# Two cross attentions by heads, an interleaved feature layout, and x's features ahead of the context's

## The chip, the cores and the metric

One core of a Trainium2 chip runs the whole program in one launch. The metric is the device time of that launch in microseconds (us). The kernel is written by hand for each engine: TensorE (PE in the profile, its weight loads PEld), VectorE (DVE), ScalarE (ACT), GpSimd (POOL, which issues the irregular transfers) and SyncE (SP, which issues the weight transfers). Engines meet at semaphores only, and each engine executes its own list of instructions in order.

## The reference, cut to what matters

256 tokens of width 2048 pass through two blocks. The first block has two layers; each projects x and a context, runs a gated attention beside a gated unit, and ends in an output product (`w_out`). In its first layer both x (2 tiles of 128 tokens) and the context (2 tiles) go through the output product; its second layer starts from the normed x:

```python
h = rms_norm(x, norm_w[layer]) * (1.0 + scale) + shift
proj = h @ w_in[layer]
...
x = x + gate * y
```

The second block has two layers, each a mixer, a cross attention to a memory of 256 tokens, and a feed-forward product with squared ReLU. The cross attention has 4 heads of width 128 (queries 2048 -> 512, outputs 512 -> 2048):

```python
x = x + memory_cross_attention(rms_norm_2(x, norm_xattn[layer]), rms_norm_2(mem, norm_mem[layer]),
                               xattn_wq[layer], xattn_wkv[layer], xattn_wo[layer])
x = x + squared_relu_mlp(rms_norm_2(x, norm_ffn[layer]), ffn_up[layer], ffn_down[layer])
```

Keys and values of the memory are computed earlier and lie ready in a DRAM buffer. Everything is float32. The large products are done with split operands: an operand is written as a rounded part (hi, of type fp32r) and the rest (lo), and a product is hi*hi + hi*lo + lo*hi, three matmuls.

## The kernel before, in words

**Weights.** All weights stream through `ring`, 8 slots of 2 x 128 rows x 512 columns (512 KB). SP loads slot u as soon as use u - 8 has been read by PE (`ring_free` for all but a product's last slot of a chunk, `gemm_full` for that one). ACT rounds a landed slot (`round_hi`, L1698), DVE subtracts (`take_lo`, L2542) and counts `w_lo`; PE waits for that count. In their instruction lists ACT and DVE do this one ring (8 uses) ahead of the use at which they stand.

**Products.** `gemm` (L917) goes chunk by chunk (512 columns of output) and, in a chunk, slot by slot; in a slot it takes every tile of 128 tokens, with the features as the stationary operand and 512 weight columns as the moving one, three matmuls for each of 2 rows of blocks. Output banks are the four `acc` banks; transposes and small products use the four `tp` banks in turn. `parts=True` makes every second slot of the first chunk wait for `feat_part`, the count of feature groups (4 of 16 blocks of 128 channels each) that are ready.

**Cross attention (`xat`, L1459, L2288, L3621).** The query product is one chunk of 8 slots for 2 tiles. After its 4th slot PE turns the last quarter of x (`turn_x`), after its 6th the keys (`turn_k`). ACT scales the two result banks by the tokens' norms into `xa_q` (L2296) and copies the turned keys. PE transposes the queries (L1476), DVE copies them to `xa_qt` (L3628). Then `attend` runs 8 units (2 token tiles x 4 heads): scores (L1048), row maximum on DVE (L2691), exponential on ACT (L1845), transposes of the probabilities (L1010), a copy on ACT (L1858), the product with the values (L1063), a scaling by the reciprocal sum on DVE. The outputs are transposed again, split by ACT (L1769) and DVE (L2616), and feed the output product `g_o`: 4 chunks of 2 slots, 2 tiles. DVE adds each chunk to x and takes the turned x of the chunk before into `feat`, the features of the feed-forward product.

**Feed-forward, upward product (`up_chunk`, L1484).** Here the weights are stationary and the features move: for each block of 128 weight columns a bank holds hi and lo of the result side by side. One matmul has 512 columns (w_hi against hi and lo of the features), one has 256 (w_lo against hi). hi and lo of `feat` are two arrays of 4096 columns each, so that the 512 columns are two runs of 256.

**From layer one to layer two of the first block.** The output product of layer one (4 tiles, 4 chunks of 8 slots) carries riders: each slot of the chunks 1 to 3 brings one more slot, of `w_mod`, which DVE sums up (L2526). In the last chunk PE turns three quarters of the new x as it stands before the norm (`turn_raw`, after the slots 2, 4 and 6); after the last slot it reduces the rider's sum (L1084), turns the last quarter and, once DVE has the diagonal of norms, spreads the norms over a bank (L1274). DVE's `x_features` (L2951) then multiplies the turned x by them (L2957), adds the shift (L2959), ACT rounds (L2063), DVE subtracts (L2591), in groups of 2, 2, 4, 4 and 4 blocks. Layer two's first product starts when the first two groups are done. ACT's list has the squares of all four tiles, then the root, before that (`sum_parts`).

Of the kernel before, what the change touches and what calls it, by code (L numbers as in the profile page):

```python
# [30 lines left out]
ACT = mybir.ActivationFunctionType  # L31
# [5 lines left out]
P = 128  # L37
# [6 lines left out]
KS = 2  # L44
# [151 lines left out]
def two_blocks(nc, I, out):  # L196
    ctx = ExitStack()
    with ctx:
# [28 lines left out]
        pairs[4096, KT * SEQ] = [feat_pair[:, j * KT * SEQ:(j + 1) * KT * SEQ] for j in range(2)]  # L227
        feat_both = feat_pair[:, :].rearrange("p (a k t) -> p a k t", a=2, t=SEQ)
# [92 lines left out]
        feat = pair(4096, KT, SEQ)  # L321
        hid_t = pair(12288, FFN // 2 // P, SEQ)
        HID = [v[:, :, :].rearrange("p b (j t) -> p b j t", t=SEQ) for v in (stage, prob)]
        rstd2 = att_s[:, 12:12 + TT]
        xn2 = view(16384, TT, D)
# [149 lines left out]
        xa_q = view(12288, TT, 512)  # L475
# [3 lines left out]
        xa_o = view(26624, TT, 512)  # L479
        xa_ot = pair(27648, 4, SEQ)  # L480

        def xat_units():
            return [dict(q=xa_qt[:, h, t * P:(t + 1) * P], k=xa_kt[:, h, :],
                         v=[xa_kv[:, j, 512 + h * HD:512 + (h + 1) * HD] for j in range(TT)],
                         out=xa_o[:, t, h * HD:(h + 1) * HD], gated=False, bias=None)
                    for t in range(TT) for h in range(4)]

# [115 lines left out]
        up_turns = []  # L603
        UP_BLOCKS = CH // P
# [277 lines left out]
        def _(pe):  # L882
# [34 lines left out]
            def gemm(g, lhs, hook=None, parts=False, late=None, between=None, each=None):  # L917
# [8 lines left out]
                def chunk(c, i, j0, s0, slots=range(g.slots)):  # L926

                    width = g.cols[c][1]
                    for s in slots:
# [9 lines left out]
                        for t in range(g.tiles):  # L939
# [266 lines left out]
            def block1(l):  # L1206
# [55 lines left out]
                def beside_out(c, s):  # L1262
                    if c == 3 and s in (2, 4, 6):
                        turn_raw(s // 2 - 1)
                    if c and s == g_out.slots - 1:
                        reduce_sum(summing[1, c])

                if l == 0:
                    gemm(g_out, feat_lhs(feat4), parts=True, each=beside_out)
                    turn_raw(3)  # L1270
# [5 lines left out]
                    tp_given["raw_ready"] += len(X_GROUPS)  # L1276
                else:
# [180 lines left out]

            def xat(l):  # L1459
                g_q, g_o = gemms[f"xat{l}"]  # L1460
                g_prev = gemms["odd" if l else "even"][-1]

                def turn_k(c, s):
                    if s != 5:
                        return
                    pe.wait_ge(sem("mem_in"), 16 * (5 + l))
                    for t in range(TT):
                        n, bank = tp_bank("act_tp")
                        for j in range(4):
# [3 lines left out]
                gemm(g_q, feat_lhs(feat), parts=True, between=(3, lambda: turn_x(g_prev, x4, 3)), each=turn_k)  # L1473
                pe.wait_ge(sem("xqk_ready"), E.due("xqk_ready"))
                for t in range(TT):
                    turn([xa_q[:, t, j * P:(j + 1) * P] for j in range(4)])  # L1476
                pe.wait_ge(sem("qkt_ready"), E.due("qkt_ready"))
                attend(xat_units())
                for t in range(TT):
                    pe.wait_ge(sem("src_ready"), E.due("src_ready"))  # L1480
                    turn_direct([xa_o[:, t, j * P:(j + 1) * P] for j in range(4)])
                gemm_to_x(g_o, feat_lhs(xa_ot), x4, parts=True)

            def up_chunk(g, c, parts, beside):  # L1484

                nonlocal q
                even = c % 2 == 0
                banks = []
                for s in range(g.slots):
                    slot = g.group(c, s)[0] % RING  # L1490
                    pe.wait_ge(sem("w_lo"), g.w0 + g.seq.index((c, s)) + 1)
                    if parts and KS * s % 4 == 0:
                        pe.wait_ge(sem("feat_part"), E.due("feat_part"))
                    for n in range(UP_BLOCKS):
                        if s == 0:
                            banks.append((None, begin("dve_free")) if even else tp_bank("tp_free"))
                        both = banks[n][1][:, :].rearrange("p (a t) -> p a t", a=2)
                        for k in range(KS):
                            kk = KS * s + k
                            w_hi, w_lo = (ring_r[:, slot, j, k, n * P:(n + 1) * P] for j in range(2))  # L1500
                            if kk == 0:
                                pe.matmul(both, w_hi, feat_both[:, :, kk, :], start=True, stop=False)  # L1502
                            mm = pe.matmul(both[:, 0], w_lo, feat_both[:, 0, kk, :], start=False, stop=False)  # L1503
                            if kk:
                                mm = pe.matmul(both, w_hi, feat_both[:, :, kk, :], start=False, stop=kk == g.kt - 1)  # L1505
                        if s == g.slots - 1:
# [2393 lines left out]
```

## Time and profile before

| | us |
|---|---|
| median of 3 runs (lowest to highest) | 3926.79 (3918.25 to 3931.02) |
| the profiled execution | 3919.9 |
| its span in the profile | 3917.9 |
| PE busy | 3774.4 (96%) |
| DVE busy | 2513.1 (64%) |
| ACT busy | 1610.7 (41%) |

The profile records one execution. Busy time of PE counts overlapping matmuls to their modelled ends, so the distance from one start to the next tells the pace, not the length of one. A timeline row is: start, length, engine, line, operation, out<-in, shape, count of merged instructions, and in brackets the idle time before it and what ended that.

### The profile page before, as it was taken

The page shows a single profiled execution, that of the slowest core. Times are in us where ns is not written, and L with a number is a line of the kernel's source. Part 1 is how long each engine was busy: PE and PEld are TensorE (multiplying, and loading weights), DVE is VectorE, ACT ScalarE, POOL GpSimd, SP SyncE. Part 2 cuts the span into 40 slices and gives each one's busy share as a digit, 9 for nine tenths or more (in the row PEclk, how much of TensorE's full clock was granted, in tenths as well). Part 3 has the DMA queues.
Part 4 walks back from the last instruction along what each step waited for, and adds up shares of the span by engine and source line. Part 5 has one row for each costly group of instructions (what it writes and reads, how often), then busy time and mean ns, then how long its engine had stood idle before and what let it go on. Part 6 is the DMA issues. An engine that isn't in the chain of part 4 may idle for free. (4 is left out here: it accounts for less than half of the span.)

```text
span 3917.9 us, 50221 instructions
## 1 busy us (share of the span) xinstructions
PE 3774.4 (96%) x20593; PEld 3052.9 (78%) x20593; DVE 2513.1 (64%) x3680; ACT 1610.7 (41%) x2274; POOL 151.8 (4%) x244
## 2 busy tenths in 40 slices
PE   7999999999999999989999999999989999999998
PEld 3688887787887887546878888888878878888887
DVE  7877786577776565766756644655496656545654
ACT  3322233324434443523445434444444554434443
POOL 2000000000000011022100000000000000000000
PEclk9999999999999999999999999999989999999999
DMA  9666564255762577244546656655645646556664
GB/s 377 231 207 202 185 196 161 81 178 155 264 204 98 190 242 222 67 152 136 179 129 183 189 193 193 190 192 189 223 143 162 218 129 190 190 193 191 189 204 156
DMA packets 352581, 722.44 MB, mean 184 GB/s; under 512 B 24064, under 2 KB 26436, under 8 KB 347488
## 3 DMA queue, kind: packets, MB, share of 16 engines
q1 hardware_dynamic: 331872, 637.74, 50.5%
q0 software_dynamic: 18784, 79.22, 5.9%
q8 instruction: 163, 2.67, 0.3%
q10 hardware_dynamic: 1696, 2.26, 0.2%
q14 instruction: 66, 0.54, 0.0%
HBM read 689.34 MB, written 26.37 MB: 183 GB/s over the span
## 5 line engine op out<-in xcount | busy, mean ns | idle before, releaser
L2542 DVE TENSOR_TENSOR ring_r<-ring,ring_r 128x1024 fp32r<-128x1024 f32 (+1 forms) x984 | 1189.0, 1217 | 1011.6 <-ACT ring_r L1698 1001.5
L1698 ACT ACTIVATE ring_r<-ring 128x1024 fp32r<-128x1024 f32 (+1 forms) x984 | 1030.9, 1054 | 1611.0 <-DMA ring<-in_w_in 412.0
L962 PE MATMUL acc<-ring_r,feat_hi 128*128 128x512 f32 x2688 | 834.9, 392 | 5.6 <-DVE feat_lo L2591 5.3
L962 PE MATMUL acc<-ring_r,hid_t_hi 128*128 128x512 f32 x2048 | 630.8, 389 | 0.0
L962 PEld LDWEIGHTS acc<-ring_r,feat_hi 128*128 128x128 f32 x2688 | 505.4, 189 | 116.2 <-issue 11.5
L962 PE MATMUL acc<-ring_r,feat_lo 128*128 128x512 f32 x1344 | 525.0, 391 | 0.0
L962 PEld LDWEIGHTS acc<-ring_r,hid_t_hi 128*128 128x128 f32 x2048 | 384.3, 188 | 79.4
L962 PE MATMUL acc<-ring_r,hid_t_lo 128*128 128x512 f32 x1024 | 398.5, 389 | 0.0
L1505 PE MATMUL tp<-feat_pair,ring_r 128*128 128x512 f32 x960 | 336.7, 394 | 0.0
L1505 PE MATMUL acc<-feat_pair,ring_r 128*128 128x512 f32 x960 | 336.4, 394 | 0.0
L962 PEld LDWEIGHTS acc<-ring_r,feat_lo 128*128 128x128 f32 x1344 | 253.7, 189 | 53.5
L1503 PE MATMUL acc<-feat_pair,ring_r 128*128 128x256 f32 x1024 | 274.0, 278 | 0.0
L1503 PE MATMUL tp<-feat_pair,ring_r 128*128 128x256 f32 x1024 | 273.9, 278 | 0.0
L962 PE MATMUL acc<-ring_r,feat_e_hi 128*128 128x512 f32 (+1 forms) x832 | 249.0, 382 | 1.1 <-DVEq L2618 1.1
L962 PEld LDWEIGHTS acc<-ring_r,hid_t_lo 128*128 128x128 f32 x1024 | 192.2, 188 | 40.0
L1505 PEld LDWEIGHTS tp<-feat_pair,ring_r 128*128 128x128 f32 x960 | 180.1, 188 | 39.3
L1505 PEld LDWEIGHTS acc<-feat_pair,ring_r 128*128 128x128 f32 x960 | 180.1, 188 | 39.0
L1503 PEld LDWEIGHTS tp<-feat_pair,ring_r 128*128 128x128 f32 x1024 | 192.4, 188 | 5.7
L1503 PEld LDWEIGHTS acc<-feat_pair,ring_r 128*128 128x128 f32 x1024 | 192.3, 188 | 5.4
L2526 DVE SCALAR_TENSOR_TENSOR big<-ring,silu_c,big 128x512 f32<-128x512 f32 x255 | 177.4, 746 | 29.0 <-DMA ring<-in_w_mod 27.9
L962 PEld LDWEIGHTS acc<-ring_r,feat_e_hi 128*128 128x128 f32 x832 | 154.1, 189 | 31.0 <-issue 1.3
L962 PE MATMUL acc<-ring_r,feat_e_lo 128*128 128x512 f32 (+1 forms) x416 | 158.8, 382 | 0.0
(520 smaller groups left out, 4395.6 us busy)
## 6 DMA issues: line engine op xcount, KB each, us to landing
ring<-in_ffn_up SPq DMA_DIRECT2D x256, 512.0 KB, 3.6
ring<-in_ffn_down SPq DMA_DIRECT2D x256, 512.0 KB, 3.6
ring<-in_w_mod SPq DMA_DIRECT2D x192, 512.0 KB, 4.8
ring<-in_w_in SPq DMA_DIRECT2D x176, 512.0 KB, 3.9
ring<-in_w_out SPq DMA_DIRECT2D x64, 512.0 KB, 3.8
ring<-in_even_w_in SPq DMA_DIRECT2D x64, 512.0 KB, 4.4
ring<-in_xattn_wkv SPq DMA_DIRECT2D x32, 512.0 KB, 4.4
ring<-in_even_w_out SPq DMA_DIRECT2D x32, 512.0 KB, 4.6
```

The source lines that it names most:

```text
L962: mm = pe.matmul(bank[0:l.shape[-1], 0:width], l, r, start=(kk == 0 and j == 0), stop=(kk == g.kt - 1 and j == len(terms) - 1))
L1503: mm = pe.matmul(both[:, 0], w_lo, feat_both[:, 0, kk, :], start=False, stop=False)
L1505: mm = pe.matmul(both, w_hi, feat_both[:, :, kk, :], start=False, stop=kk == g.kt - 1)
L1698: f(ring_r[:, slot, 0, 0:kt, 0:width], ring[:, slot, 1, 0:kt, 0:width], ACT.Copy) \
L2526: op = stt(v, w, by, v, ALU.mult, ALU.add)
L2542: tt(lo, raw, hi, ALU.subtract).then_inc(sem("w_lo"), E.up("w_lo"))
```

## The change

Three edits.

1. **Layout.** `feat` now holds hi and lo of a block of channels side by side: 16 blocks of (hi 256, lo 256). The 512 moving columns of the upward product are one run.
2. **Cross attention by heads.** The query product has the weights stationary, as the upward product has (`turned_block`): four banks, one for each head, come out as head x tokens, hi beside lo. The first four slots are done for all heads; from then on head by head (slots 4 to 7 of head 0, then 1, 2, 3), with the scores of heads 0 and 1, the transposes of head 0's probabilities and so on placed between. Query copies and transposes go away; the norms of the tokens enter as the exponential's scale. Scores of a head lie for both tiles in one `tp` bank; maximum, reciprocal and scaling are done for both tiles, the scaling on the probabilities. The product with the values has the values stationary, so that its output is already turned. The output product starts with slot 0 of its chunks 0 and 1, which need heads 0 and 1 only.
3. **x ahead of the context.** In the last chunk of layer one's output product, slots 4 to 7 are done for x's tiles first, and then for the context's. The remaining turns of x, the rider's sum, the norms and `x_features` are placed between the context's slots on PE, and between the weights' groups on ACT and DVE; the shift goes into ACT's rounding (as its bias) and into DVE's subtraction, one block of 256 columns at a time. The context's norm diagonal moves to the start of layer two.

```diff
-        feat_both = feat_pair[:, :].rearrange("p (a k t) -> p a k t", a=2, t=SEQ)
+        feat_both = feat_pair[:, :].rearrange("p (k a t) -> p k a t", a=2, t=SEQ)
...
+        feat = Pair(feat_both[:, :, 0], feat_both[:, :, 1], view(4096, KT, 2, SEQ)[:, :, 1])
+        feat_hl = feat_pair[:, :].rearrange("p (k n) -> p k n", n=2 * SEQ)
...
-            g.append(Gemm(f"xq{l}", W("xattn_wq_2", l), D, chunks(0, 512), 2, "act_free"))
+            g.append(Gemm(f"xq{l}", W("xattn_wq_2", l), D, chunks(0, 512), 4, "dve_free"))
```

PE, the product used by the queries and by the upward product:

```diff
+            def turned_block(g, bank, c, s, n, parts=False):
...
+                for k in range(KS):
+                    kk = KS * s + k
+                    w_hi, w_lo = (ring_r[:, slot, j, k, n * P:(n + 1) * P] for j in range(2))
+                    if kk == 0:
+                        pe.matmul(bank[:, :], w_hi, feat_hl[:, kk, :], start=True, stop=False)
+                    mm = pe.matmul(bank[:, 0:SEQ], w_lo, feat.hi[:, kk, :], start=False, stop=False)
+                    if kk:
+                        mm = pe.matmul(bank[:, :], w_hi, feat_hl[:, kk, :], start=False, stop=kk == g.kt - 1)
```

PE's order in a cross attention (`both` is 4, `heads` is 0 to 3; `out_part(c, s, t)` is chunk, slot and tile of the output product):

```diff
+                for s in range(both):
+                    for n in heads:
+                        queries(n, [s])
+                turn_x(g_prev, x4, 3)
+                queries(0, range(both, both + 2))
+                turn_k()
+                queries(0, range(both + 2, g_q.slots))
+                queries(1, range(both, g_q.slots))
+                score(0)
+                queries(2, range(both, g_q.slots))
+                score(1)
+                queries(3, range(both, both + 2))
+                turn_prob(0)
+                queries(3, range(both + 2, g_q.slots))
+                score(2)
+                outputs(0)
+                turn_prob(1)
+                score(3)
+                outputs(1)
+                turn_prob(2)
+                x_at[g_o] = ("dve_free", given["dve_free"])
+                out_part(0, 0, 0)
+                out_part(0, 0, 1)
+                outputs(2)
+                out_part(1, 0, 0)
+                turn_prob(3)
+                out_part(1, 0, 1)
+                outputs(3)
+                for c in range(g_o.n):
+                    for s in range(1 if c < 2 else 0, g_o.slots):
+                        for t in range(TT):
+                            out_part(c, s, t)
+                    if c:
+                        turn_x(g_o, x4, c - 1)
```

ACT's list is, in order: `weights(0, 1, 2)`, `k_turned`, `q_low(0)`, `weights(3)`, `q_low(1)`, `weigh(0)`, `q_low(2)`, `weigh(1)`, `prob_turned(0)`, `q_low(3)`, `out_hi(0)`, `prob_turned(1)`, `weigh(2)`, `weigh(3)`, `out_hi(1)`, `prob_turned(2)`, `weights(4)`, `out_hi(2)`, `prob_turned(3)`, `weights(5)`, `out_hi(3)`, `weights(6, 7)`. Here `weights` rounds slots of the output product, `q_low` copies the lo half of a head's query bank, `weigh` is the exponential of a head (two calls of 256 columns), `prob_turned` copies the turned probabilities, `out_hi` rounds a head's output.

DVE's list is: `weights(0, 1, 2)`, `query(0)`, `weights(3)`, `query(1)`, `greatest(0)`, `weighed(0)`, `query(2)`, `greatest(1)`, `weighed(1)`, `query(3)`, `greatest(2)`, `out_lo(0)`, `greatest(3)`, `weighed(2)`, `out_lo(1)`, `weighed(3)`, `weights(4)`, `out_lo(2)`, `weights(5)`, `out_lo(3)`, `weights(6, 7)`. `query` adds the two halves of a bank, `greatest` is the maximum and its scaling, `weighed` the reciprocal sum and the two multiplications of the probabilities.

The last chunk of layer one's output product, on PE:

```diff
+                    order = [(s, range(g.tiles), True) for s in slots]
+                    if apart and c == g.n - 1:
+                        s_apart, groups = apart
+                        order = order[:s_apart] + [(s, ts, ts is groups[-1]) for ts in groups for s in range(s_apart, g.slots)]
...
+                        if not last:
+                            continue
...
+                    if s in (2, 3, 4):
+                        turn_raw(s - 2)
+                    if s == 4:
+                        reduce_sum(summing[1, 3])
+                        turn_raw(3)
+                    if s == 5:
+                        x_rows()
```

and on DVE, with the groups of `x_features`, one for each `next(groups)`:

```diff
+                    if s == 4:
+                        x_turned(1)
+                        add_tiles(c, range(TT))
+                        x_turned(2)
+                        take_sum(summing[1, 3])
+                        x_turned(3)
+                        norm_diag(TT, diag4)
+                    if s >= 4 and s < 7:
+                        next(groups)
...
+                def rest(i):
...
+                    for j in range(k, k + n):
+                        d, name = feat4.at(j, 1, slice(0, SEQ)), "feat_part" if i and j == k + n - 1 else "dve_step"
+                        stt(d.lo, d.raw, mod_col(1, 0, 0)[:, j:j + 1], d.hi, ALU.add, ALU.subtract).then_inc(sem(name), E.up(name))
...
+                scaled(0)
+                scaled(1)
+                rest(0)
+                rest(1)
+                yield
+                scaled(2)
+                scaled(3)
+                rest(2)
+                yield
+                scaled(4)
...
+                rest(3)
+                yield
+                rest(4)
+                yield
```

ACT has the squares of x's last part and the root for x at slot 4, before the rounding of the first two groups; the next two groups at slot 5, the last at slot 6; the root for the context follows after the product.

## Rows read from the trace of the kernel before

**Rows 1.** The page, part 1: busy us, share of the span, instructions.
```profile
PE 3774.4 (96%) x20593; PEld 3052.9 (78%) x20593; DVE 2513.1 (64%) x3680; ACT 1610.7 (41%) x2274; POOL 151.8 (4%) x244
```

**Rows 2.** Waits of PE: line, releaser, us in total, times, longest.
```profile
PE tp L1010 <- ACTq L2300: 9.6, 2, 4.8
PE acc L962 <- DVE feat_lo L2591: 5.3, 1, 5.3
```

**Rows 3.** Stretches: length; busy PE, PEld, DVE, ACT, POOL; granted clock; DMA share; GB/s.
```profile
922.00:936.00 14.00, 4.78 (x32) 4.18 (x31) 13.55 (x22) 8.96 (x24) 0.00 (x0) 0.63 0.23 75
...
1984.00:2008.00 24.00, 23.95 (x116) 19.67 (x113) 15.54 (x19) 13.09 (x23) 0.00 (x0) 1.00 0.53 174
2008.00:2035.00 27.00, 17.63 (x81) 13.45 (x82) 13.29 (x38) 12.95 (x32) 0.00 (x0) 0.75 0.06 22
3150.00:3176.00 26.00, 16.76 (x80) 12.42 (x80) 13.27 (x38) 12.94 (x32) 0.00 (x0) 0.80 0.07 24
```

**Rows 4.** PE's timeline, first cross attention.
```profile
1984.09 11.17 PE L962 MATMUL acc<-ring_r,feat_pair 128*128 128x512 f32 x48
1995.10 1.03 PE L1010 MATMUL tp<-ident,big 128*128 128x128 f32 x8
1995.89 5.71 PE L962 MATMUL acc<-ring_r,feat_pair 128*128 128x512 f32 x24
...
2026.13 0.70 PE L1063 MATMUL acc<-big,prob_t 128*128 128x128 f32 x4
2026.67 0.60 PE L1048 MATMUL acc<-big 128*128 128x256 f32 x2
2027.10 0.43 PE L1010 MATMUL tp<-ident,prob 128*128 128x128 f32 x2
...
2034.84 1.08 PE L962 MATMUL acc<-ring_r,xa_ot_hi 128*128 128x512 f32 x2 [1.80 <-DVEq L2618]
...
2060.91 0.47 PE L1502 MATMUL acc<-feat_pair,ring_r 128*128 128x512 f32 x1
```

**Rows 5.** PE's timeline, first and last edge of the second cross attention.
```profile
3126.10 11.15 PE L962 MATMUL acc<-ring_r,feat_pair 128*128 128x512 f32 x48
...
3200.69 0.48 PE L1502 MATMUL acc<-feat_pair,ring_r 128*128 128x512 f32 x1
```

**Rows 6.** PE's timeline from layer one to layer two.
```profile
922.30 1.84 PE L1084 MATMUL tp<-ones,big 128*128 128x2 f32 x16
...
928.95 1.22 PE L1274 MATMUL tp<-big 128*128 128x128 f32 x4 [3.87 <-DVEq L2586]
935.52 1.19 PE L962 MATMUL acc<-ring_r,feat_hi 128*128 128x512 f32 x2 [5.35 <-DVE feat_lo L2591]
...
948.27 0.62 PE L962 MATMUL acc<-ring_r,feat_hi 128*128 128x512 f32 x2
...
948.95 0.62 PE L962 MATMUL acc<-ring_r,feat_hi 128*128 128x512 f32 x2
```

**Rows 7.** PE's timeline, upward product: two starts in a row, and its first half's end.
```profile
2084.06 0.40 PE L1505 MATMUL acc<-feat_pair,ring_r 128*128 128x512 f32 x1
2084.30 0.40 PE L1502 MATMUL tp<-feat_pair,ring_r 128*128 128x512 f32 x1
...
2240.09 0.62 PE L962 MATMUL acc<-ring_r,hid_t_hi 128*128 128x512 f32 x2
```

**Rows 8.** Groups by form: busy us, mean ns of one, idle before.
```profile
L1845 ACT ACTIVATE prob<-acc,att_s 128x256 f32<-128x256 f32 x8 | 3.8, 472 | 5.2 <-DVE att_s L2491 5.2
L1845 ACT ACT_TABLE_LOAD x1 | 1.3, 1283 | 4.2 <-PE acc L1048 4.2
...
L2542 DVE TENSOR_TENSOR ring_r<-ring,ring_r 128x1024 fp32r<-128x1024 f32 x16 | 19.1, 1222 | 9.6 <-ACT ring_r L1698 9.6
L2691 DVE TENSOR_REDUCE att_s<-acc 128x1 f32<-128x256 f32 x8 | 3.4, 424 | 3.6 <-PE acc L1048 3.3
...
L3356 DVE SCALAR_TENSOR_TENSOR big<-prob,big 128x256 f32<-128x256 f32 x16 | 7.8, 485 | 0.6
```

More of the change, by code:

```diff
@@ L1468, in turn_k @@
                         n, bank = tp_bank("act_tp")
-                        for j in range(4):
+                        for j in heads:
                             mm = pe.transpose(bank[:, j * P:(j + 1) * P], xa_kv[:, t, j * P:(j + 1) * P], ident[:, :])
                         to_act(n, mm)
[L1473 to L1476, printed above, removed]
@@ L1494, in up_chunk @@
                     for n in range(UP_BLOCKS):
[L1495 to L1505, printed above, removed]
@@ L2289, in xat, with weights, k_turned @@
                 g_q, g_o = gemms[f"xat{l}"]
[L2291 to L2292 removed]
+                def weights(*slots):
+                    for s in slots:
+                        round_hi(g_q.group(0, s)[0] + RING)
+                def k_turned():
+                    for t in range(TT):
                         f(xa_kt[:, :, t * P:(t + 1) * P], take_turn()[:, :].rearrange("p (k t) -> p k t", t=P), ACT.Copy) \
                             .then_inc(sem("act_tp"), E.up("act_tp"))
[L2296 to L2297 removed]
@@ L3180, in add_gated, with add_tiles @@
                 def add_gated(c, i):
-                    for t in range(tiles):
+                    add_tiles(c, range(TT, 4) if c == 3 and not l else range(tiles))
+                    if l and c:
+                        turn_part(feat_e, c - 1, "norm_mix0")
+                def add_tiles(c, ts):
+                    for t in ts:
                         bank = take("gemm_full")
@@ L3631, in xat, with weights, query @@
-                dve.wait_ge(E.last_sem(), E.last_count())
-                dve.nop().then_inc(sem("qkt_ready"), E.count("qkt_ready"))
-                attend(xat_units())
-                for t in range(TT):
-                    dve.nop().then_inc(sem("src_ready"), E.up("src_ready"))
-                lo_direct(xa_ot, TT, (0,))
+                def weights(*slots):
+                    for s in slots:
+                        take_lo(g_q.group(0, s)[0] + RING)
+                def query(n):
+                    bank = take("gemm_full")
+                    dve.wait_ge(sem("sq_ready"), E.due("sq_ready"))
+                    tt(xa_qt[:, n], bank[:, 0:SEQ], stage[:, n % 2, 0:SEQ], ALU.add).then_inc(sem("dve_free"), E.up("dve_free"))
@@ new lines, in out_lo @@
+                def out_lo(h):
+                    dve.wait_ge(sem("hi_ready"), E.due("hi_ready"))
+                    E.seen["pv_full"] += 1
+                    tt(xa_ot.lo[:, h], tp[out_tp[h + 4 * l]][:, 0:SEQ], xa_ot.hi[:, h], ALU.subtract).then_inc(sem("tp_free"), E.up("tp_free"))
+                turn_skip(2)
+                weights(0, 1, 2)
+                query(0)
+                weights(3)
+                query(1)
+                greatest(0)
+                weighed(0)
+                query(2)
@@ L3637, in xat @@
+                greatest(1)
+                weighed(1)
+                query(3)
+                greatest(2)
+                out_lo(0)
+                greatest(3)
+                weighed(2)
+                out_lo(1)
+                weighed(3)
+                weights(4)
+                out_lo(2)
+                weights(5)
+                out_lo(3)
+                weights(6, 7)
+                turn_skip(4)
+                t_n += 8
                 residual(g_o, feat, f"norm_ffn{l}")
```

266 lines of the change are left out of this document (183 added, 83 removed).

## The prediction

> **What bounds the kernel now.** The page comes first: PE is busy for 96% of the span, DVE for 64%, ACT for 41% [rows 1]. So time can only go where PE waits, runs at the lower clock, or does work that can be left out. The waits of PE come next, because 4% of 3918 us is some 150 us spread over the kernel: among the long ones are the two waits for the turned queries, 4.8 us each, and one of 5.3 us for the first features of layer two [rows 2]. Then the stretches around these places [rows 3]: from 2008 to 2035, the middle of the first cross attention, PE is busy for 17.6 of 27 us, its granted clock averages 0.75 of 2.4 GHz (that is, part of the time at 1.2 GHz), and hardly any weights are moved (22 GB/s); the second attention looks the same (16.8 of 26). From 922 to 936, the change of layers, PE is busy for 4.8 of 14 us at a mean clock of 0.63, while DVE works for 13.55: there DVE's chain bounds. The reader is to see that in both places the wait is a chain of small steps across engines, with no product beside it. The timelines give the edges.
>
> **The cross attentions.** From the query product's first matmul to the feed-forward's first it is now 2060.91 - 1984.09 = 76.8 us [rows 4] and 3200.69 - 3126.10 = 74.6 us [rows 5]. What PE has to do there after the change:
> - Query product: 64 pairs of a 512- and a 256-column matmul. The upward product does such pairs: 512 of them and one turn of 0.8 us from 2060.91 to 2240.09 [rows 4, 7], which is 0.348 us each. 22.3 us. (Now: 96 matmuls; 48 take 11.0 us [rows 4], so 22.0. The turned form costs 0.3 more.)
> - Turns of x (8 transposes, 1995.10 to 1995.89, 0.79 us [rows 4]), four in all (three follow the output chunks), and of the keys, the same: 4.0 us.
> - Scores: 8 calls of 256 columns, 0.43 us each (2026.67 to 2027.10 [rows 4]): 3.4 us. As many as now.
> - Transposes of probabilities: 16, as now: 1.8 us, a little over the pace of the turns.
> - Values: 8 calls of 256 columns in place of 16 of 128 (two take 0.54, 2026.13 to 2026.67 [rows 4]); I take the price of a score: 3.4 us.
> - Output product: 96 matmuls. In undisturbed stretches three take 0.68 (948.27 to 948.95 [rows 6]): 21.8 us.
> The turns of the queries and of the outputs go. Sum: 56.7 us of PE work. The best case is no wait at all: -20.1 and -17.9.
>
> Now the waits that are left, each followed through both lists, in us after the first matmul. PE ends four slots at 11.1, the turn of x at 12.0, head 0's slots 4 and 5 at 13.4, the keys at 14.2. The last feature group was ready 2.5 us after the turn's end in the rows' manner of working, at 14.5: PE waits 0.3. Head 0 is done at 15.9, head 1 at 18.7. ACT has by then three roundings (0.96 us apart), the keys and the low half, DVE three subtractions (1.22 [rows 8]) and the sum at about 18.5: the scores of head 0 follow at once. Maximum on DVE (two of 0.42 [rows 8], in one instruction), then the table load (1.28 [rows 8]) and two exponentials of 0.47 with their accumulators, then reciprocal and two multiplications on DVE (0.42 to 0.49 for 256 columns [rows 8]): probabilities at 25.2. PE, which has head 2, the scores of head 1 and half of head 3 to do, is there at 24.8: it waits 0.5. From there the product is used up and the softmax of the other heads goes on between small steps: 0.4 before the outputs of head 0, 1.0 before those of head 1 (their bank is freed by head 2's exponential, which stands behind two copies on ACT), 0.3 and 0.3 around the first slots of the output product, and 1.2 before its second slots, which need DVE's `out_lo(3)`, queued behind a rounding and a subtraction of weights. That is 4.0 us. I add 1.5 for some fifteen changes between small and large products (the first matmul after a turn starts some 0.1 late). Result: 62.2 us for each attention, so -14.6 and -12.4.
>
> What these waits hold up: DVE's waiting `greatest` and `weighed` stand ahead of the weights of the output product, but only slots 4 to 7 of it, which PE reads 12 us later. After the attention DVE has the same work for each output chunk as now, at the same distance behind PE, and the first weights of the upward product can be loaded as soon as the output product's first slot is read, before PE is there.
>
> Between its waits PE keeps doing products, none of the waits is over 1.2 us, and the clock in the trace fell only where PE had waited 3.9 us and more [rows 2, 3, 6]; so I take 2.4 GHz throughout. The loss of now (0.75 over 27 us) goes with the waits and is in the 76.8.
>
> One price has a second source. The Trainium skill (ScalarE: Activation LUTs, What ACT_TABLE_LOAD costs) puts a change of tables at 1283 ns and a drain of about 1380 more. The row has 1283 [rows 8], and the exponential follows it in the trace without a further pause, so the measurement decides. By the skill's figure one load an attention would cost up to 1.4 us more, 2.8 in the sum.
>
> **x ahead of the context.** Now PE ends the chunk's products at 922.30, starts layer two at 935.52, waiting 3.87 and 5.35 between, and the first matmuls there run at the lower clock; slot 4 of that product starts at 948.27 [rows 6]. After the change PE's order in the last chunk is: slots 4 to 7 for x (48 matmuls, 10.9 us, from 899.6, which is 922.3 less 96 matmuls and one turn, to 910.5), then slot 4 for the context, turn, sum (1.7), turn, to 916.4; slot 5 to 919.1; the spread norms 0.9; slots 6 and 7 to 925.6. Behind this DVE adds x's tiles at 911.9, turns, and has the diagonal at 918.3, in time; ACT's squares and root are done at 915. The features of the first two groups are ready at about 923.2 (ACT rounds 256 columns in some 0.3 us; DVE's fused subtraction is 0.485 alone [rows 8], near 0.4 in a row), the first weights at 924.4. So layer two starts at 925.6, with a warm clock: 9.9 us earlier. DVE is then late: two multiplications of 1.2 us, four blocks, two weight subtractions for slots 2 and 3 (PE waits 0.5); then `rest(3)`, the context's two additions with theirs (2.75 us) and only then the weights of slot 4, at 939.7, where PE stands since 937.1. From 948.27 to 939.7: -8.6 us. After that DVE is some 6 us behind where it would have been ahead, but the next need is 10 us off. The bounds: nothing of the 2.6 and 0.5 waits, -11.7; twice as much, -5.5. The ring slots 4 to 7 are held up to 9 us longer; the loads that take their place land about 4 us after their release and are needed 10 us later: nothing.
>
> **The layout.** The trace before doesn't show a product with one run of 512 feature columns. Two starts of the upward product's 512-column matmuls lie 0.24 us apart (2084.06 to 2084.30 [rows 7]), and the pair of 0.348 is 0.007 above 1.5 times 0.227 [rows 6]. If all of that belonged to the split into two runs, 2048 such matmuls would give back up to 14 us. But here also the operands' roles are swapped, and a 256-column matmul leaves little time for the next weight load. A loss is bounded by the same 14 us: nothing in the rows speaks for one. [...] I take zero, because the rows leave other causes, and keep the 14 as a rival.
>
> **Sum.** -14.6 - 12.4 - 8.6 = -35.6 us. Against the profiled execution's 3919.9 that is 3884.3. The median of the runs shown is 3926.8, 6.9 higher; the forecast is for a median: 3926.8 - 35.6 = **3891 us**. Its own range, with the bounds of its terms (57 to 66 us an attention, -5.5 to -11.7): 3881 to 3903.
>
> **Rivals.**
> - The split runs were the upward product's surcharge: 12 of the 14 us come back, 3879. For it: 0.24 against 0.227 where no small matmul is near. Against: swapped roles. Chance 0.2.
> - The softmax doesn't fit between the products. ACT's and DVE's lists are in order, and a head's chain has seven hops; if each hop costs 0.5 us more than I took, the four heads cost some 8 us an attention: 62.2 becomes 70, the sum -20, 3907. For it: in the 27 us of now ACT and DVE are busy for 13 each while PE waits for one or the other [rows 3], so the hops count. Against: now nothing else runs beside the chain. 0.15.
> - The gain is taken back elsewhere (the context's features or the weights' queue late in layer two, later waits growing as the products move up): under 0.3% is left. 0.05.
> - Slower. The short waits of 0.3 to 1.2 us come close together in the attentions, and PE is granted 1.2 GHz from the first of them (25 us in) to the upward product. The rest of an attention is 34 us of PE work; at half the clock it costs 34 more. Two attentions give +68 against -35.6: 3959. It decides from 18 us of work at the lower clock in each. For it: 0.75 over 27 us now. Against: that followed a wait of 4.8 us [rows 2], and by 2026.67 a score takes 0.43 again, half of what it would at 1.2 GHz [rows 4]. 0.04.
> - The change doesn't overlap what it says (a count that makes a head wait for a later one): 3915 or so, within the third case.
>
> **Chances.** Forecast 0.56, the others 0.2, 0.15, 0.05, 0.04. 0.3% is 12 us, about what a measurement of this kernel tells from no change: faster 0.91, same 0.05, slower 0.04. The range takes in the first two rivals: 3873 to 3909.
>
> **What would show it.** Right: from the query product's first matmul to the upward product's first some 62 us twice; no wait of PE over 1.5 us between; granted clock near 1 there; layer two's first product right behind the context's last slot, with one wait of 2 to 3 us for `w_lo` at its slot 4. The upward product's 512-column matmuls: 0.24 apart as now, or near 0.227 (the first rival). Wrong: PE waits of 2 us and more for `src_ready`, `pv_full` or the bank of the outputs; a granted clock of 0.5 in the output product.

## The result and the profile after

| | before | after |
|---|---|---|
| median of 4 runs each (lowest to highest), us | 3927.7 (3918.3 to 3931.0) | 3892.0 (3886.0 to 3895.1) |
| ratio, 95% interval | | 0.9912 (0.9895 to 0.9928) |
| the profiled execution / its span | 3919.9 / 3917.9 | 3893.6 / 3891.5 |

The kernel became faster by 35.7 us between the medians; by the interval of the ratio, by 28 to 41. The two profiled executions differ by 26.3 only; where the other 9 went is the first question below. Part 1 of the page of after, beside [rows 1]:

```profile
PE 3760.1 (97%) x20593; PEld 3044.3 (78%) x20593; DVE 2507.7 (64%) x3674; ACT 1612.1 (41%) x2285; POOL 151.7 (4%) x244
```

PE is busy for 14 us less, although one stage at a lower clock added some 9 to it (below). The waits of PE that belong to the changed places (line, releaser, us in total, times, longest), beside [rows 2]:

```profile
PE acc L960 <- DVE ring_r L2699: 4.4, 3, 2.1
PE acc L1477 <- DVE big L2823: 3.9, 2, 2.0
PE tp L1532 <- ACT prob L2423: 2.0, 2, 1.0
PE acc L1550 <- DVE xa_ot_lo L3845: 1.9, 2, 1.0
PE acc L1550 <- issue: 1.1, 2, 0.5
PE acc L1478 <- DVE feat_pair L2748: 0.2, 1, 0.2
```

The 9.6 us for turned queries and the 5.3 for the first features are gone. The second line is new, and no step of the prediction has it: L1477 is the first matmul of a block, L2823 the addition of the attention's output to x. Stretches of the first attention, columns as in [rows 3]:

```profile
1982.60:2008.00 25.40, 25.24 (x150) 21.98 (x149) 16.81 (x29) 15.35 (x32) 0.00 (x0) 1.00 0.32 105
2008.00:2020.00 12.00, 10.45 (x54) 8.54 (x53) 6.38 (x17) 6.97 (x19) 0.00 (x0) 1.00 0.53 177
2020.00:2035.00 15.00, 14.03 (x68) 11.38 (x67) 8.93 (x11) 7.13 (x12) 0.00 (x0) 1.00 0.43 139
```

Granted clock 1.00 throughout, where it was 0.75 over 27 us [rows 3], and the softmax now stands inside the weights' traffic. PE's timeline there, beside [rows 4]:

```profile
1982.61 0.48 PE L1477 MATMUL acc<-feat_pair,ring_r 128*128 128x512 f32 x1
...
1993.96 1.04 PE L1010 MATMUL tp<-ident,big 128*128 128x128 f32 x8
...
2007.68 0.60 PE L1010 MATMUL tp<-ident,prob 128*128 128x128 f32 x4
...
2013.71 1.10 PE L1532 MATMUL tp<-prob_t,big 128*128 128x256 f32 x4 [1.01 <-ACT prob L2423]
...
2015.79 0.70 PE L1550 MATMUL acc<-ring_r,xa_ot_hi 128*128 128x512 f32 x2 [0.54 <-issue]
...
2018.63 1.02 PE L1532 MATMUL tp<-prob_t,big 128*128 128x256 f32 x4
2019.30 0.81 PE L1550 MATMUL acc<-ring_r,xa_ot_hi 128*128 128x512 f32 x2
...
2024.71 0.74 PE L1550 MATMUL acc<-ring_r,xa_ot_hi 128*128 128x512 f32 x2 [0.97 <-DVE xa_ot_lo L3845]
...
2043.80 0.47 PE L1477 MATMUL acc<-feat_pair,ring_r 128*128 128x512 f32 x1
...
2047.43 0.50 PE L1477 MATMUL acc<-feat_pair,ring_r 128*128 128x512 f32 x1 [1.97 <-DVE big L2823]
```

From the first query matmul to the upward product's first it is 2043.80 - 1982.61 = 61.2 us (76.8 before). The second attention, beside [rows 5]:

```profile
3110.76 0.47 PE L1477 MATMUL acc<-feat_pair,ring_r 128*128 128x512 f32 x1
...
3171.65 0.47 PE L1477 MATMUL acc<-feat_pair,ring_r 128*128 128x512 f32 x1
...
3175.20 0.50 PE L1477 MATMUL acc<-feat_pair,ring_r 128*128 128x512 f32 x1 [1.90 <-DVE big L2823]
...
3177.07 0.63 PE L1480 MATMUL acc<-feat_pair,ring_r 128*128 128x512 f32 x1
3177.50 0.41 PE L1478 MATMUL acc<-feat_pair,ring_r 128*128 128x256 f32 x1
```

60.9 us (74.6 before). Here the wait of 1.90 is followed by matmuls of 0.63 us that start 0.43 before the next: 1.2 GHz, for 3.4 us by the granted clock (0.72 over the 6 us behind the wait). The change of layers, beside [rows 6]:

```profile
889.70 1.03 PE L1010 MATMUL tp<-ident,big 128*128 128x128 f32 x8
...
910.56 1.03 PE L1010 MATMUL tp<-ident,big 128*128 128x128 f32 x8
911.43 1.84 PE L1084 MATMUL tp<-ones,big 128*128 128x2 f32 x16
913.14 1.07 PE L1010 MATMUL tp<-ident,big 128*128 128x128 f32 x8
...
916.80 0.60 PE L1266 MATMUL tp<-big 128*128 128x128 f32 x4
...
929.96 0.73 PE L960 MATMUL acc<-ring_r,feat_hi 128*128 128x512 f32 x2 [1.66 <-DVE ring_r L2699]
...
937.83 0.73 PE L960 MATMUL acc<-ring_r,feat_hi 128*128 128x512 f32 x2 [2.14 <-DVE ring_r L2699]
```

Layer two starts without a wait (at about 922.6, where the context's last 24 matmuls end) and waits at its slots 2 and 4. The turn after the last chunk's slot 2 stands at 892.39 before and 889.70 after, so slot 4 is 937.83 - 889.70 = 48.1 us behind that turn, where it was 948.27 - 892.39 = 55.9: 7.8 us less. Read to the start of that layer's output product (the next two fences) it is 8.3.

**Where the two profiles lose 9 us of it.** One line of a tile (its matmuls, then the first and the last start): `featb` is read by the output product of layer two, `feat_e` from the even stage's first product to the last before the first attention. Before, then after:

```profile
L962 PE MATMUL acc<-ring_r,featb_hi x256: 387/389/476, 1268.7 to 1357.3; 128*128 128x512 f32 x128
L962 PE MATMUL acc<-ring_r,feat_e_hi x832: 227/389/775, 1358.5 to 1982.8; 128*128 128x512 f32 x154, 128*128 128x144 f32 x13
```

```profile
L960 PE MATMUL acc<-ring_r,featb_hi x256: 387/389/476, 1257.7 to 1346.2; 128*128 128x512 f32 x128
L960 PE MATMUL acc<-ring_r,feat_e_hi x832: 227/389/776, 1347.5 to 1981.4; 128*128 128x512 f32 x154, 128*128 128x144 f32 x13
```

After is 11.0 us ahead at 1358, and 1.4 at 1983: the unchanged even stage took 633.9 us in place of 624.3. The windows that start at the same place of it (before, then after) show why: with the granted clock at 0.56, PE gets through 26 matmuls in the 20 us in place of 44.

```profile
1750.00:1770.00 20.00, 19.68 (x44) 8.13 (x45) 17.96 (x47) 1.88 (x3) 3.73 (x7) 1.00 0.12 34
```

```profile
1739.00:1759.00 20.00, 19.37 (x26) 6.09 (x26) 13.36 (x41) 2.39 (x4) 3.90 (x8) 0.56 0.14 36
```

Ten more profiles were taken with the experiments. The even stage took 624.4 (layout), 634.0 (x_ahead), 633.2 (attention), 634.0 (no_interleave), 633.8 (after_again), 626.1 (bank_first), 631.1 (dve_order), 626.9 (out_order), 624.3 (all_three), 627.1 (after_third). So it comes and goes with single executions: after itself shows 634, 634 and 627, and up to that point attention differs from before by the layout alone, as layout does, which is without it. Whether an edit makes it more frequent, twelve profiles don't tell. A comparison of two profiles is blind to 10 us unless each stage is compared by itself.

### The profile page after: what moved, and what is told of

Its sections match the earlier page's. It is cut to its first block and busy times, and to the rows that moved or that the text cites. A ratio compares the mean times of both kernels' runs of the same rounds, so it can differ in the third digit from the quotient of the medians.

```text
span 3891.5 us, 50287 instructions
## 1 busy us (share of the span) xinstructions
PE 3760.1 (97%) x20593; PEld 3044.3 (78%) x20593; DVE 2507.7 (64%) x3674; ACT 1612.1 (41%) x2285; POOL 151.7 (4%) x244
## 5 line engine op out<-in xcount | busy, mean ns | idle before, releaser
L1480 PE MATMUL acc<-feat_pair,ring_r 128*128 128x512 f32 x1080 | 380.4, 395 | 0.0
L1478 PE MATMUL acc<-feat_pair,ring_r 128*128 128x256 f32 x1152 | 310.3, 280 | 0.3 <-DVE feat_pair L2748 0.2
L1480 PEld LDWEIGHTS acc<-feat_pair,ring_r 128*128 128x128 f32 x1080 | 203.2, 188 | 43.6
L1478 PEld LDWEIGHTS acc<-feat_pair,ring_r 128*128 128x128 f32 x1152 | 217.3, 189 | 6.7 <-issue 0.7
```

Source lines behind the costliest of these rows:

```text
L1478: mm = pe.matmul(bank[:, 0:SEQ], w_lo, feat.hi[:, kk, :], start=False, stop=False)
L1480: mm = pe.matmul(bank[:, :], w_hi, feat_hl[:, kk, :], start=False, stop=kk == g.kt - 1)
```

## The experiments

Each was timed in five rounds beside the kernel before; us are the ratio times 3925. All compute the whole reference.

**layout**: the kernel before with the feed-forward features interleaved, and nothing else.

```diff
-                                pe.matmul(both, w_hi, feat_both[:, :, kk, :], start=True, stop=False)
+                                pe.matmul(both[:, :], w_hi, feat_hl[:, kk, :], start=True, stop=False)
```

> The kernel before with the layout alone: hi and lo of each block of feature channels side by side, so that the upward product's 512 columns are one run. Theory (layout gives nothing): the pair of a 512- and a 256-column matmul stays at 0.35 us, the first half's upward product at 179.2 us, the time at 3927.7 within 0.2%. Rival (the two runs were the upward product's surcharge): the pair at 0.34 us, 3 us less for each of the four upward halves, the time at about 3916.

Measured: ratio 0.9993 (0.9982 to 1.0003), -3 us (-7 to +1). The first half's upward product takes 2063.33 to 2242.5 = 179.2 us, as before (2060.91 to 2240.09). The rival's 12 us are outside the interval: the layout gives nothing that shows.

**x_ahead**: the kernel before with the hunks of the third edit alone (`apart`, `beside_out`, `x_features`, `sum_parts`).

> The kernel before with x's features ahead of the context's alone. Theory (the step is worth what the two traces show between the turn after slot 2 and layer two's slot 4, and nothing of it is taken back): 8 us less, 3919 to 3920. Rival one (the later stages take it back: DVE is behind at the start of layer two, or the stage that ran at the lower clock between 1730 and 1760 us in the trace after does so because of this step): 0 to 3 us less, and PE granted 1.2 GHz in that stage here too. Rival two (the loss in that stage comes with single executions, whatever the kernel): that stage at 1.2 GHz in some profiles of this series and at 2.4 in others.

Measured: 0.9976 (0.9967 to 0.9985), -9 us (-13 to -6). The same two waits (1.67 and 2.10), and nothing is taken back: from the turn after slot 2 to the first `featb` matmul it is 376.1 to 376.4 us in the three kernels without the step and 367.9 to 369.1 in the seven profiles with it as it stands, 8.1 less on average. The even stage at the lower clock was here too, but that is rival two, as the list above shows.

**attention**: the kernel before with the first two edits (layout and attention by heads), x not ahead.

> The kernel before with the cross attentions by heads (and the layout that they use) alone. Theory (the attentions give what the two traces show: 76.8 to 61.2 and 74.6 to 60.9 us, less a new wait of 1.9 us in each upward product): 25.3 us less, about 3902. Rival one (the prediction's terms, no new wait): 27 us less, 3901 or under. Rival two (the medians moved by 9 us more than the two profiles because the attentions are worth more than one profile shows): 33 us less, 3895.

Measured: 0.9937 (0.9921 to 0.9954), -25 us (-31 to -18). The attentions take 61.1 us each, with the same waits (1.0, 1.0, 0.5, and 1.87 and 1.91 in the upward products). The theory's number is met; the interval excludes the 33 of rival two, and doesn't tell 25.3 from the prediction's 27. The traces do: there the new wait stands. With x_ahead's -9 the two halves of the change add up to the -34 of the whole.

**no_interleave**: the kernel after, heads 2 and 3 of the queries before the first scores.

```diff
                 queries(1, range(both, g_q.slots))
+                queries(2, range(both, g_q.slots))
+                queries(3, range(both, g_q.slots))
                 score(0)
-                queries(2, range(both, g_q.slots))
                 score(1)
-                queries(3, range(both, both + 2))
                 turn_prob(0)
-                queries(3, range(both + 2, g_q.slots))
                 score(2)
```

> The kernel after with PE's order in the attentions undone in one point: heads 2 and 3 of the query product are finished before the first scores, so that the first softmax has no product beside it. Theory (interleaving is worth the waits that it covers: 4.6 us before head 0's transposes and about 1 before its outputs, at full clock): 5.7 us longer in each attention, 3892 + 11 = 3903. Rival one (after a wait of 4 to 5 us PE is also granted 1.2 GHz for some 10 us of work, as in the kernel before): 10 to 12 us in each, about 3914. Rival two (the gain of the attentions is that of the removed turns and of the scaling, not of the interleaving): less than 2 us in each, 3895.

Measured: 0.9945 (0.9930 to 0.9960), 3904.6 us in the median, 12.6 more than after. PE's timeline in the first attention, and the window behind the wait:

```profile
2007.16 1.89 PE L1516 MATMUL tp<-big 128*128 128x256 f32 x8
2011.25 0.66 PE L1010 MATMUL tp<-ident,prob 128*128 128x128 f32 x4 [2.20 <-DVE prob L2647]
2011.74 1.19 PE L1516 MATMUL tp<-big 128*128 128x256 f32 x4
2014.10 2.08 PE L1532 MATMUL tp<-prob_t,big 128*128 128x256 f32 x4 [1.17 <-ACT prob_t L2431]
...
2049.70 0.48 PE L1477 MATMUL acc<-feat_pair,ring_r 128*128 128x512 f32 x1
```

```profile
2012.00:2020.00 8.00, 6.67 (x20) 4.50 (x18) 3.83 (x13) 4.34 (x13) 0.00 (x0) 0.57 0.09 34
```

The attentions take 67.2 us (from 1982.55) and 65.0, that is 6.0 and 4.1 more. The total is near the theory's 11, but its parts are not the theory's: the waits are 2.2 and 1.2 us in place of 4.6 and 1, and in the first attention the granted clock is 0.57 over the 8 us behind them, which is rival one's mechanism at a smaller size. So of the 29 us that the two attentions gained, 10 hang on this order, and 19 remain with no product beside the first softmax. What these 19 are no run separates; the traces show what went along. The waits of PE come to 9.3 and 9.5 us in the attentions of before, 5.5 and 6.2 here, 2.7 and 2.5 in after. The stretches at 1.2 GHz come to 17.1 and 10.2 us before, 6.8 and 0 here, none in after, and cost at most half of themselves. So waits make up nearly half of the 29 us, and the clock much of the rest.

**after_again** and **after_third**: the kernel after, repeated beside the others.

> The kernel after, once more, with a new profile. Theory one (the stretch at 1.2 GHz in the mixer of layer one, 9.6 us, comes with single executions of any of these kernels: it was there in the profiles with x ahead, with the attentions alone, without interleaving and after, and not in those of before and of the layout alone): the stretch from the even stage's first product to the first cross attention takes 624 or 634 us here, and the time is about 3892. Rival (the changed kernels have it always, and then the change's gain in the other stages is larger than its median shows): 634 again.

> The kernel after, beside the run of the three reorderings on the same chip: 3891 within 0.2%; its new profile has the mixer stretch of layer one at 624 to 627 or at 631 to 634 us, whichever.

Measured: 3891.3 and 3885.7 us, ratios 0.9919 (0.9906 to 0.9932) and 0.9907 (0.9891 to 0.9923). The even stage took 634 and then 627: the first theory holds. With the first comparison that makes a mean ratio of 0.9913, 34 us.

**bank_first**: the kernel after, DVE's list at the end of an attention.

```diff
+                    if not (early and c == g.n - 1):
+                        adds(c)
                     if dst and c:
                         turn_part(dst, c - 1, scale)
+                    if early and c == g.n - 2:
+                        adds(c + 1)
```

> The kernel after, with one change: DVE adds the last chunk of the attention's output product to x before it subtracts the weights of the chunk before. Theory (the upward product's third block waits 1.9 us for its bank only because two weight subtractions of 1.2 us stand ahead of the additions on DVE): both waits of 1.9 us go, and with the second one the 3 us at a lower clock behind it; 4 to 5.5 us less, about 3887. Rival (DVE is full in that stretch, so the wait only moves to the weights or the last features of the upward product): 0 to 2 us less.

Measured: 0.9904 (0.9886 to 0.9922), 3882.1 us. DVE's timeline in after, where the last chunk's additions (L2823 at 2046.70) stand behind two subtractions of weights, and PE waits until 2047.43:

```profile
2042.87 1.29 DVE L2748 TENSOR_TENSOR feat_pair<-big,feat_pair 128x512 fp32r<-128x512 f32 x2
2044.42 2.36 DVE L2699 TENSOR_TENSOR ring_r<-ring,ring_r 128x1024 fp32r<-128x1024 f32 x2 [0.25 <-ACT ring_r L1793]
2046.70 1.28 DVE L2823 TENSOR_TENSOR big<-big,acc 128x512 f32<-128x512 f32 x2
```

and the same place in bank_first, where PE starts the third block at 2038.26 with no wait:

```profile
2035.92 1.29 DVE L2748 TENSOR_TENSOR feat_pair<-big,feat_pair 128x512 fp32r<-128x512 f32 x2
2037.13 1.28 DVE L2821 TENSOR_TENSOR big<-big,acc 128x512 f32<-128x512 f32 x2
2038.33 2.35 DVE L2699 TENSOR_TENSOR ring_r<-ring,ring_r 128x1024 fp32r<-128x1024 f32 x2
```

Both waits are gone from the trace, no other took their place, and the granted clock stays at 1.00 there; so the rival falls and the cause is shown. The size is shown by the trace only: the first halves of the upward products take 179.2 and 179.2 us, in after 181.2 and 182.7, so 5.6 less. The medians' difference to after is inside the spread of the runs.

**dve_order**: the kernel after, the lists at the change of layers (DVE's hunks; ACT rounds the groups in the same new order, and takes the context's root after layer two's first slots).

```diff
                 scaled(2)
+                yield
+                rest(2)
                 scaled(3)
-                rest(2)
                 yield
+                rest(3)
                 scaled(4)
...
-                    add_tiles(c, range(TT, 4) if c == 3 and not l else range(tiles))
+                    if l or c < 3:
+                        add_tiles(c, range(tiles))
...
+                    held_lo(g_out)
                     next(groups)
-                    held_lo(g_out)
+                    add_tiles(3, range(TT, 4))
```

> The kernel after, with DVE's and ACT's lists at the change of layers reordered: the weights of layer two's slots 2 to 7 stand ahead of the feature groups needed later, and the context's additions, root and diagonal come last. Theory (the waits of 1.66 us before slot 2 and 2.14 before slot 4 are a matter of order; DVE has 2.3 us of idle time in that stretch): 0.3 left of both, 3.5 us less, about 3888. Rival (DVE is full until the second chunk, so that PE waits there for the context's banks or for the weights of slot 8): under 1 us less.

Measured: 0.9905 (0.9889 to 0.9920), 3886.9 us. PE has no wait left between 880 and 960 us, and from the turn after slot 2 to the first `featb` matmul it is 364.2 us, against 368.0 in after: 3.8 less. The theory (3.5 us) holds: DVE wasn't full there, its list and ACT's were in the wrong order. The medians alone couldn't tell it from after.

**out_order**: the kernel after, the end of the attentions (PE's hunk; on ACT `out_hi(1)` also moves ahead of `weigh(3)` and `prob_turned(3)` ahead of `out_hi(2)`, and on ACT and DVE `weights(5)` behind head 3's output).

```diff
                 out_part(0, 0, 1)
+                turn_prob(3)
                 outputs(2)
                 out_part(1, 0, 0)
-                turn_prob(3)
+                outputs(3)
                 out_part(1, 0, 1)
-                outputs(3)
```

> The kernel after, with the end of the attentions reordered: the transposes of head 3's probabilities before the outputs of head 2, so that the outputs of head 3 have a part of the output product behind them; on ACT the rounding of head 1's output before head 3's exponential. Theory (the waits of 0.54 us before the first slots and 0.97 before the second slots are the chain PE, ACT, DVE, PE with nothing beside it): both go, 3.0 us less over two attentions, about 3889. Rival (they are the place in ACT's and DVE's lists, behind a rounding and a subtraction of weights, and come back at another head): under 1 us less.

Measured: 0.9917 (0.9901 to 0.9933), 3889.8 us. The attentions take 59.7 and 59.8 us, 1.2 less each. The wait of 0.97 is gone, that of 0.54 stayed though ACT rounds head 1's output at once:

```profile
2006.24 1.10 PE L1532 MATMUL tp<-prob_t,big 128*128 128x256 f32 x4 [1.01 <-ACT prob L2423]
2007.18 0.60 PE L1010 MATMUL tp<-ident,prob 128*128 128x128 f32 x4
2008.32 0.70 PE L1550 MATMUL acc<-ring_r,xa_ot_hi 128*128 128x512 f32 x2 [0.54 <-issue]
```

So the theory is half right. This wait is the bare chain, product, rounding, subtraction, next product, with only four transposes beside it. PE's order up to it is the same in both kernels, and ACT rounds head 1's output as soon as the product is done in both (2014.85 in after), so the order on ACT and DVE isn't its cause. Whether one more product between on PE would cover it was not run.

**all_three**: bank_first, dve_order and out_order together.

> The kernel after with the three reorderings together (bank_first, dve_order, out_order). Theory (each removes waits at its own place, and with the bank free in time nothing takes the end of the attentions back): 3.8 + 1.0 + 3.5 + 2.4 us of waits, up to 3 more where the wait for the bank was followed by the lower clock; 11 to 13 us less than after, about 3879 in a median. Rival (the shorter waits add up on DVE, which is full at the end of the attention, so that the bank is late again): 5 to 8 less, about 3885.

Measured: 0.9883 (0.9863 to 0.9903), 3877.0 us, the fastest kernel of the study: 46 us (38 to 54) under before, and by the ratios 12 us (3 to 20) under after. The interval doesn't part the theory's 11 to 13 from the rival's 5 to 8; the trace does. From the turn after slot 2 to the first `featb` matmul it is 364.7 us, the attentions take 59.7 and 59.9 and the first halves of the upward products 179.1 each: some 11.6 less than in the trace of after. Of the waits listed for after, 1.0 and 0.5 in each attention, the 0.2, and 0.4 of the first line are left.

## Why the prediction was right, point by point

- **The sum.** -35.6 was forecast and -35.7 measured between the medians, -34 over three comparisons. That it agrees to 0.1 is luck: in the two traces the changed places give -32.0 (last point). The bounds of the prediction's own terms add up to 3878 and 3902, not to its 3881 and 3903; the result lies in both.
- **The attentions' work** was 58.2 us with the switches. Measured: 61.2 less waits of 2.7 is 58.5. The calls for scores and values were priced too high where a product follows (0.86 a head; it starts 0.67 later, 2018.63 to 2019.30; where another small step follows it is 0.86 to 0.93), and the first four slots too low (32 pairs from 1982.61 to 1993.96, 0.355 each).
- **The attentions' waits.** 4.0 forecast, 2.7 found. The bank of head 1's outputs was right to the figure (1.0). The wait for head 0's probabilities (0.5) didn't come: PE was there 25.1 us after the first matmul, DVE had finished at 23.4. The wait before the second slots (1.2, measured 0.97) was right in size and wrong in cause: it was given to a rounding and a subtraction of weights in the way, but ACT's rounding of the output started when PE's product allowed, and DVE took it 0.1 us after that. It went when another product stood in the chain (out_order).
- **The step that failed** is "after the attention DVE has the same work for each output chunk as now, at the same distance behind PE", from which no wait followed. The work is the same, the distance is not. Before, DVE starts the last chunk's additions 0.85 us after PE has left that chunk for the turn (0.88 in the second attention):

```profile
2060.12 1.04 PE L1010 MATMUL tp<-ident,big 128*128 128x128 f32 x8
2060.97 1.28 DVE L2666 TENSOR_TENSOR big<-big,acc 128x512 f32<-128x512 f32 x2
```

  In after it is 3.7 us (2043.01 to 2046.70), and it has been 3.6 since chunk 1:

```profile
2030.33 1.03 PE L1010 MATMUL tp<-ident,big 128*128 128x128 f32 x8
2032.75 1.23 DVE L2699 TENSOR_TENSOR ring_r<-ring,ring_r 128x1024 fp32r<-128x1024 f32 x1 [2.92 <-ACT ring_r L1793]
2033.89 1.28 DVE L2823 TENSOR_TENSOR big<-big,acc 128x512 f32<-128x512 f32 x2
```

  As slot 0 of the chunks 0 and 1 is done ahead, PE ends chunk 1 only 2.7 us after chunk 0, while DVE's additions for it stand behind weights of the upward product that ACT can round at 2031.66 only, when they have landed. Later chunks take DVE 6.4 us and PE 6.3, so the distance stays. This is read from the traces; bank_first moved only the last chunk's additions. The third block of the upward product needs the bank of that chunk's first tile 1.5 us after the product starts (2036.78 to 2038.26 in bank_first), so PE waits 1.97 and 1.90 us. From start to end, the first half of an upward product takes 179.1 to 179.2 us in the ten cases without the wait, 181.1 to 181.4 in seven with it, and 182.6 to 182.9 in the seven where the granted clock is 0.72 over the 6 us behind it: the wait costs 2.1 us, and the clock 1.5 more. The attentions' term is therefore -15.6 - 13.7 + 2.0 + 3.6 = -23.7 in place of -27.0.
- **The clock.** "the clock in the trace fell only where PE had waited 3.9 us and more" misreads the rows: behind the wait of 1.80 us at 2034.84 two matmuls take 1.08 us [rows 4], where two take 0.62 in [rows 6], and the granted clock is 0.50 from 2035.0 to 2038.4. So a fall behind a short wait was to be seen before, and it came behind the new one.
- **x ahead**: -8.6 forecast, -7.8 at slot 4 and -8.3 by the output product. Its start was right within 0.3 us (925.6 forecast, less the 2.7 that the trace of after is ahead by then; 922.6 measured). The mis-sized term is the small operations: ACT's rounding of a block took 0.41 us (four in 1.71), not 0.3, and DVE's fused subtraction 0.42. Eight such roundings, 3.31 us, stand on ACT ahead of slot 2's weights, and DVE waits 0.65 and 0.88 us for ACT there. The wait at slot 2 became 1.66 (forecast 0.5), and the one at slot 4 2.14 (2.6); this link is read from the trace. The Trainium skill (ScalarE: Activation LUTs, What ACT_TABLE_LOAD costs) has a price for it: with a bias per partition 280 ns plus 0.833 a column, about 93 less back to back. By this the estimate is 400 ns for 256 columns; the trace agrees, with 0.41 us.
- **The layout**: nothing was forecast, and nothing that shows was measured.
- **The rivals.** Of the softmax that doesn't fit, only its order-dependent part exists (no_interleave). Slower by the clock: no stretch of the attentions fell below 1.00. Its mechanism was seen on a small scale in no_interleave and behind the new wait.
- **The table load** takes 1283 ns, as in [rows 8], and stands in front of the wait for the first maximum, so it costs nothing; of the further 1380 ns of the Trainium skill (same page and section) nothing is seen. The exponential starts 0.38 us after the load, when DVE's maximum has come.
- **Where the rest is.** By stages, after less before in the two traces: -2.7 to the turn after slot 2, -8.3 from there to the output product of layer two, +9.5 in the even stage, -15.6 and -13.7 in the attentions, +2.0 and +3.6 in the first halves of the upward products, -1.2 in all the rest; together -26.4. The changed places give -32.0. Of the -2.7, 1.5 arise near 420 us and 1.2 between 640 and 690, where the granted clock is 0.91 and 0.90 before and 0.96 and 0.93 after: stages that nobody changed. Open is why the kernels with x ahead reach that turn at 888.8 to 890.5 us in all but one profile (892.0 in all_three) and the three without it at 892.4 to 894.9.

## What to carry to other kernels

Put a chain of small steps between products rather than behind them: the order alone gave a third of the attentions' gain here, by covered waits and the clock behind them. When a stage shrinks, follow each result bank through the helper engine's list across the stage's end: the next wait was a bank freed 2 us late, by two weight subtractions that nobody needed for 10 us. When part of a product is done ahead, its chunks end closer together, and the engine that takes them over may fall behind. Compare traces stage by stage, from a landmark just ahead of the change to one just behind, never by their ends.

## What the runs showed of the hardware

An unchanged stage of 624 us took 631 to 634 in six of twelve profiles; in all six PE had one stretch of 17 to 20 us at a granted clock near 0.5 (26 matmuls in 20 us in place of 44) behind waits of up to 3.8 us that all twelve have. And a single wait of 1.9 us between full-rate products was followed by 3.4 us at 1.2 GHz in seven cases out of fourteen, and by 2.4 GHz in the other seven. In the three executions of after it was each time the second attention's wait and never the first's, in no_interleave it was both, in out_order the first; what decides is not shown. A short wait has therefore two prices, here 2.1 and 3.6 us.
